# The head of a fused attention kernel: the first weight block in two transfers, the token rows ahead of the last two blocks, half a product of zeros less

## What is computed

```python
def _rmsnorm(x, g):
    y = x32 * lax.rsqrt(jnp.mean(x32 * x32, axis=-1, keepdims=True) + RMS_EPS)
    return (y * g).astype(x.dtype)

xn = _rmsnorm(x, norm_pre)                      # x: 520 rows of 1024
(qa, kvc, kvs, kvw, gn, ga, qd, kvd, krp, gb, ma, mb) = jnp.split(xn @ w_in, IN_OFFSETS, axis=-1)
...
cmp_past = cache_nsa_cmp[l, page_table]         # 8 x 4096 cached rows of 256 keys and values
kc, vc = _compress(jnp.concatenate([cmp_past, kvc], axis=1), pe_cmp)   # means over blocks of 32 rows
```

## Time and profile before

| | before |
|---|---|
| median of 3 runs | 666.37 us (666.15 to 666.65) |
| profiled execution | 666.29 us |
| its span | 664.5 us |
| PE busy | 650.8 us (98%) |
| DVE busy | 446.0 us (67%) |
| ACT busy | 214.4 us (32%) |
| POOL busy | 77.6 us (12%) |
| moved by DMA | 179.44 MB, mean 270 GB/s |

### The profile page before, as it was taken

The page is one execution under the profiler, slowest core; times in us unless marked ns, Lnnn a source line. Parts: engine busy times, 40 slices in busy tenths (PEclk is TensorE's granted clock), DMA queues, the critical chain, the costliest instruction groups (busy, mean ns, idle before and its releaser), DMA issues.

```text
span 664.5 us, 15351 instructions
## 1 busy us (share of the span) xinstructions
PE 650.8 (98%) x5771; PEld 433.3 (65%) x5771; DVE 446.0 (67%) x1234; ACT 214.4 (32%) x586; POOL 77.6 (12%) x89
## 2 busy tenths in 40 slices
PE   8999999999999998999999999999999999999996
PEld 3444444463466775778777676688788888886443
DVE  2198799676677778866575664637585757648866
ACT  0311321686445455544453542421011111010221
POOL 0344334126000000220201000000000000000010
PEclk9999999999999999999999999999999999999998
DMA  8999999999989999978759789975411112018011
GB/s 332 417 425 422 423 427 403 353 379 273 366 277 381 400 399 412 408 276 326 279 177 373 276 318 359 406 270 222 159 64 64 64 49 78 1 70 343 3 64 63
DMA packets 67587, 179.44 MB, mean 270 GB/s; under 512 B 7513, under 2 KB 16498, under 8 KB 60218
## 3 DMA queue, kind: packets, MB, share of 16 engines
q1 hardware_dynamic: 56088, 125.14, 51.2%
q0 software_dynamic: 8640, 48.90, 18.2%
q10 hardware_dynamic: 2786, 4.42, 1.8%
HBM read 169.38 MB, written 12.72 MB: 274 GB/s over the span
## 4 chain that ended last, share of the span: by engine, by line
PE 88%; DVE 5%; DMA 3%; ACT 2%; issue 1%; SPq 1%; DVEq 0%; ACTq 0%
PE bank L1561 20%; PE bank L978 12%; PE bank L1398 9%; PE bank L1612 7%; PE bank L1259 5%; PE bank L1382 4%; PE bank L1285 4%; PE bank L1269 4%; PE bank L1367 4%; DMA projP<-x 3%; PE bank L1590 2%; PE bank L1142 2%; PE bank L1332 2%; PE bank L1342 1%; PE bank L1220 1%
## 5 line engine op out<-in xcount | busy, mean ns | idle before, releaser
L978 PE MATMUL bank<-W,XG 128*128 128x494 f32 x192 | 83.6, 580 | 0.7 <-DVE projP L1998 0.7
L1871 ACT ACTIVATE projP<-bank,projP 128x128 f32<-128x128 f32 (+3 forms) x96 | 49.8, 525 | 38.5 <-DVE projP L2354 37.8
L2657 DVE TENSOR_TENSOR projP<-projP,bank 128x260 f32<-128x260 f32 x81 | 32.6, 422 | 42.4 <-PE bank L1561 41.6
L1398 PE MATMUL bank<-W 128*128 128x260 f32 x256 | 60.3, 389 | 0.0
L1661 ACT ACTIVATE projP<-bank 128x128 f32<-128x128 f32 (+5 forms) x87 | 33.4, 392 | 82.2 <-PE bank L1561 47.7
L978 PEld LDWEIGHTS bank<-W,XG 128*128 128x128 f32 x192 | 35.2, 192 | 36.5 <-issue 35.0
L1398 PEld LDWEIGHTS bank<-W 128*128 128x128 f32 x256 | 47.3, 190 | 10.6 <-issue 3.5
L1661 ACT ACTIVATE W<-bank 128x512 f32<-128x512 f32 (+2 forms) x69 | 40.2, 582 | 38.3 <-PE bank L1021 13.3
L2354 DVE CUSTOM_DVE_ANT_0 bank<-bank,maskb 128x128 f32<-128x128 f32 (+3 forms) x96 | 45.6, 509 | 8.0 <-PE bank L1259 7.1
L1259 PE MATMUL bank<-W 64*128 64x128 f32 (+7 forms) x192 | 46.0, 466 | 0.7 <-ACT projP L1871 0.7
L821 POOL DMA_INDIRECT ring<-cmp,idxi x32 | 38.6, 1208 | 67.8 <-DVE VV L2065 48.1
(11 more groups left out here) (479 smaller groups left out, 1163.6 us busy)
## 6 DMA issues: line engine op xcount, KB each, us to landing
ring<-latent SPq DMA_DIRECT2D x168, 256.0 KB, 4.9
XG<-latent SPq DMA_DIRECT2D x56, 256.0 KB, 4.4
W<-w_gate SPq DMA_DIRECT2D x12, 1024.0 KB, 5.8
W<-w_attn SPq DMA_DIRECT2D x16, 494.0 KB, 12.2
W<-latent SPq DMA_DIRECT2D x20, 256.0 KB, 5.3
rope_rows<-ring SPq DMA_DIRECT2D x16, 256.0 KB, 4.4
ring<-win SPq DMA_DIRECT2D x8, 512.0 KB, 7.7
ring<-w_out SPq DMA_DIRECT2D x2, 2048.0 KB, 11.8
```

The costliest lines, as they stand in the source:

```text
L978: mm = pe.matmul(bank[2 * (u % 2) + n][:, 0:GW], XG[:, k * TOK + tl * P:k * TOK + (tl + 1) * P], w_part(half, k, n), start=(k == 0), stop= ...
L1398: mm = pe.matmul(bank[6][:, 0:HALF], gate_w[g % 2][:, at:at + P], X2[:, k * TOK + hf * HALF:k * TOK + (hf + 1) * HALF], start=(k == 0), st ...
L1871: act.activation(Pb[u % 4][:, 0:w], bank[u % 2][:, 0:w], ACT.Exp, bias=NMp[:, u:u + 1], scale=-1.0, accum_out=RSp[:, u:u + 1]).then_inc(S[ ...
L2657: dve.tensor_tensor(out, a, pair_bank(v, product)[:, 0:HALF], ALU.add).then_inc(S["z_by_dve"], 1)
```

## The change

It has four parts.

1. SP loads block 0 of the first half in two transfers, group 0 on `w_in0` and group 1 on a semaphore `apart_in`, and PE takes block 0 by columns: group 0 for both tiles, then, after a wait on `apart_in`, group 1 for both tiles. The other blocks keep their order.
2. SP issues `xtok` and `xdec` ahead of blocks 6 and 7.
3. The second product on zeros is 256 words wide and not 512.
4. The late rotary loads count on `apart_in` too (the old `rope_apart`), one step of 16 further on.

```diff
@@ rope_landed
-                eng.wait_ge(S["rope_apart"], 16 * (ROPE_APART.index(p2) + 1))
+                eng.wait_ge(S["apart_in"], 16 * (ROPE_APART.index(p2) + 2))
@@ SP
-                sp.dma_start(W[:, k * 2 * GW:(k + 1) * 2 * GW], t["w_attn"][:, k, 0:2 * GW]).then_inc(S[f"w_in{k}"], 16)
-            sp.dma_start(xtok.rearrange("p (t c) -> p t c", t=TILES), t["x"][0:SEQ].rearrange("(t p) c -> p t c", p=P)).then_inc(S["xtok_in"], 16)
-            sp.dma_start(xdec[0:DEC], t["x"][SEQ:TOK]).then_inc(S["xtok_in"], 16)
+                if k == 6:
+                    sp.dma_start(xtok.rearrange("p (t c) -> p t c", t=TILES), t["x"][0:SEQ].rearrange("(t p) c -> p t c", p=P)).then_inc(S["xtok_in"], 16)
+                    sp.dma_start(xdec[0:DEC], t["x"][SEQ:TOK]).then_inc(S["xtok_in"], 16)
+                if k == 0:
+                    sp.dma_start(W[:, 0:GW], t["w_attn"][:, 0, 0:GW]).then_inc(S["w_in0"], 16)
+                    sp.dma_start(W[:, GW:2 * GW], t["w_attn"][:, 0, GW:2 * GW]).then_inc(S["apart_in"], 16)
+                else:
+                    sp.dma_start(W[:, k * 2 * GW:(k + 1) * 2 * GW], t["w_attn"][:, k, 0:2 * GW]).then_inc(S[f"w_in{k}"], 16)
@@ PE, project_first
-                    for tl in range(2):
-                        for n in range(2):
-                            mm = pe.matmul(bank[2 * tl + n][:, 0:GW], XG[:, k * TOK + tl * P:k * TOK + (tl + 1) * P],
-                                           w_part(0, k, n), start=(k == 0), stop=(k == KM - 1))
-                        if k == KM - 1:
+                    for tl, n in ((0, 0), (1, 0), (0, 1), (1, 1)) if k == 0 else ((0, 0), (0, 1), (1, 0), (1, 1)):
+                        if (k, tl, n) == (0, 0, 1):
+                            pe.wait_ge(S["apart_in"], 16)
+                        mm = pe.matmul(bank[2 * tl + n][:, 0:GW], XG[:, k * TOK + tl * P:k * TOK + (tl + 1) * P],
+                                       w_part(0, k, n), start=(k == 0), stop=(k == KM - 1))
+                        if k == KM - 1 and n == 1:
                             mm.then_inc(S["p1"], 1)
@@ PE, ahead of project_first
-            for _ in range(2):
-                pe.matmul(bank[7][:, :], VV[:, 0:P], VV[:, 0:512], start=True, stop=True)
+            for width in (512, 256):
+                pe.matmul(bank[7][:, 0:width], VV[:, 0:P], VV[:, 0:width], start=True, stop=True)
```

More of the change, by code:

```diff
@@ L1817, in load_rope @@
                     act.wait_ge(S["rope_out1"], 128)
-                act.dma_start(rope_home(p2), rope_rows[p2 * P:(p2 + 1) * P]).then_inc(S["rope_apart" if p2 in ROPE_APART else "kr_landed"], 16)
+                act.dma_start(rope_home(p2), rope_rows[p2 * P:(p2 + 1) * P]).then_inc(S["apart_in" if p2 in ROPE_APART else "kr_landed"], 16)
             group_copied(act, 15)
```

## The result

| | before | changed |
|---|---|---|
| median of the first measurement | 666.51 us (4 runs) | 675.79 us (4 runs, 673.31 to 680.66) |
| ratio, 95% interval | | 1.0128 [1.0086, 1.017] |
| median of a second one (experiment 12) | 665.96 us (11 runs) | 671.78 us (7 runs, 670.71 to 679.79) |
| ratio, 95% interval | | 1.0074 [1.0049, 1.01] |
| profiled execution | 666.29 us | 674.48 us |

The forecast was 668.3 us with a range up to 669.9. The direction and the mechanism came out as forecast. The size did not: the medians differ by 5.8 and 9.3 us and not by 2.0. The ratios are those on record with their intervals; they are not the quotients of the medians (1.0087 and 1.0139), so read them as one estimate and the medians as another. The changed kernel scatters by 7 to 9 us.

What follows compares the result with a forecast made beforehand. PE's list was taken as the path, with DMA full for the first 115 us. Late gathers eat the head's 1.1 us gain and leave PE 2.0 us behind: 666.29 + 2.0 = 668.3 us, range 666.4 to 669.9.

Steps and rivals of the forecast that it cites:

- The row that decides: POOL's first gather waits for block 7; with block 7 landing at 25.1 it is issued at 26.0, not 20.87.
- The stall at the first eviction: PE's 0.85 us wait before project(2) at 34.06, claimed to go once the token rows come earlier.
- 1 to 3: Expected profile sign: PE waits about 1 to 3 us for DVE at the second average, near 56 to 58.
- the head's gain holds: Rival: the gathers keep in time, idle time under 1.5 us or so, and the run takes 665.2; chance 0.10.
- slow clock at the second average: Rival: a 2 us wait there could lower PE's clock, giving 669.5 to 671; chance 0.10 together with longer idle time.
- I take 3.8: DMA engines idle from 24.3 until the first gather packets: 3.2 to 4.5 us, taken as 3.8.
- The sum had stretched 3.8 to 5.8 us for the 13th gather: q0 moves 0.55 of 0.85 MB beside the second weight half, so the gather lands at 73.1 to 74, not 67.3.
- the 2.8 us that I read from the earlier trace: Time from POOL's first gather issue (20.87) to first packet on q0 (about 23.7); the other bound was 1.5 us.
- the forecast's own step: At the fifth average PE takes the 20th fold, ended at 96.7, at about 96.8 against 94.84: 2.0 us behind.
- Sum on PE's head: 0.25 + 0.85 = 1.1 us: PE's start: 0.25 us from an earlier block 1 start plus 0.85 us of first eviction stall removed.
- The rotary table ... 5.5 us of cover of which 2 are used. Then PE is dense to the end: Late loads: table lands at 142.95, DVE reads it at 148.41, so no further loss; PE's 2.0 us stays.
- 1.5 to 2 us if the whole of block 0 runs so: Clock rival's price at the head: with fewer zeros, block 0's products run at 1.2 GHz; chance 0.10 with longer idle.

Runs made afterwards that it cites:

- experiment 12: The changed kernel as it is, timed and profiled once more against the kernel before: 671.78 us, ratio 1.0074.
- experiment 3: The whole change, with POOL's first gather waiting for block 5 and not block 7, against the kernel before: 667.19 us, 1.0005.
- experiment 4: The kernel before, with POOL also waiting for the token rows before its first gather and no transfer moved: 673.57 us, 1.009.
- experiment 6: The kernel before with token rows ahead of blocks 6 and 7 and the first gather waiting for block 5: 665.91 us, 0.9987.
- experiment 7: The kernel before with token rows ahead of blocks 6 and 7, gathers waiting for block 5, second zeros product 256 words: 666.79 us, 0.9995.
- experiment 8: The whole change, with w_qup and w_k issued ahead of the second rope_out, against the kernel before: 670.57 us, 1.0065.
- experiment 5: The kernel before with token rows ahead of blocks 6 and 7 and the first gather waiting for block 6: 673.85 us, 1.0092.
- experiment 1: The kernel before with only the token rows moved ahead of blocks 6 and 7: 673.93 us, 1.0104.
- experiment 9: The whole change, w_qup and w_k ahead of the second rope_out, second average three blocks later, against the kernel before: 672.44 us, 1.0069.
- experiment 11: The kernel before with only w_qup and w_k issued ahead of the second rope_out: 667.3 us, 0.9998.
- experiment 10: The kernel before with token rows ahead of blocks 6 and 7, gathers waiting for block 5, w_qup and w_k before second rope_out: 665.53 us, 0.9969.
- experiment 2: The kernel before with only block 0 split and taken by columns; token rows last, zeros whole: 667.39 us, 0.9998.

## Why the prediction failed in size

**What held.** The row that decides was the right one: the first gather waits for block 7, forecast for 26.0 and found at 26.79; the empty stretch was forecast at 24.5 to 28 and found at 25.4 to 28.5. The stall at the first eviction went. PE waits for folds at the second average, 2.7 us for the "1 to 3" forecast. Experiments 3 and 4 show this cause from both sides. The rival "the head's gain holds" needed an idle time under 1.5 us, which never came; with the gathers early (3, 6, 7) PE leaves the head 0.2, 0.4 and 1.3 us ahead, and the times stay within their noise of before. The rival "slow clock at the second average" came true in the first trace, on top of the forecast and not in place of it.

**The term mis-sized first: "I take 3.8" of idle time.** The idle time itself was not too short: the engines stop at about 25.3, and the first packets of the gather come at 28.5, 1.7 us after its issue, so 3.2 us, the lower end that I had given. Three things were missing beside it. The gathers start slowly: of the 0.73 MB by which the lag grows from 28.0 to 35.0 us, 0.21 belong to the last 0.5 us of idle time, and 0.52 to this, 1.2 us of transfer. The hardware queue ebbs before it is empty: from 21.0 to 25.4 us the lag grows by 0.37 MB, 0.9 us. And the split cost 0.17 MB, 0.4 us. The lag is 3.2 + 1.2 + 0.9 + 0.4 = 5.7 us, where the sum worked with 3.8. The sum had stretched 3.8 to 5.8 us for the 13th gather, by the share of q0; by the same share 5.7 us give 8.8, and the 13th is used 8.2 us late (75.53 against 67.33). The Trainium skill puts the first byte of a gather at about 1 us (DMA: Bandwidth & Descriptors, "Specifications"); 1.7 us with 1.0 us of issue in it is nearer to it than to the 2.8 us that I read from the earlier trace rows, where q0 had to share with a full q1. None of my rows had the slow start. That fewer gathers stand issued at the start, one and not four, is the difference at hand; no run shows it as the cause.

**What follows from it.** The 16th fold ends at 86.2 (forecast 84.2) and the 20th at 98.7 (forecast 96.7). By the forecast's own step PE can take the 20th at 98.7 to 98.8 in place of 94.84, which is +3.9 and not +2.0. The second trace of the changed kernel shows just that, +3.9. The rule was right and its input 2 us short. At the second average PE was already 3.2 us behind, above the 2.0 that the sum took from the fifth.

**The step on the head: "Sum on PE's head: 0.25 + 0.85 = 1.1 us".** The 1.1 us never came: PE goes into `project(2)` 0.44 us behind in the first trace and 0.67 in the second (34.73). The sum had block 1 unmoved at 8.55 and the second half at about 5.5. They landed at 10.1 and 6.57. The first 7.9 us moved 0.24 MB less than before (the sums of the two rows of GB/s). I had counted bytes; a row of half a block is 1976 bytes and not 3952, and block 0 takes two such rows for each one. The traces show the loss with the split; that the size of the rows makes it, and not the second issue, is argued. The split costs the head 1.1 us on average (experiment 7), as much as the whole gain forecast for it. So the first eviction came at 33.1 and not at 31.4, and DVE's first fold at 33.79 and not 1.5 us early. Here this didn't set the result, because the averages waited anyway.

**The step that failed: "The rotary table ... 5.5 us of cover of which 2 are used. Then PE is dense to the end".** I checked one transfer of SP's shifted chain and not the one ahead of it. `w_k` lands just when it is wanted. (SP's transfers are q1 in the profile; ACT's are a queue of their own, q10.) Of the ten traces without the edit of experiment 8, ACT waits for it in seven, and in the four with the edit in none. In six of those seven the copy follows the issue by 11.07 to 11.33 us; in the seventh by 13.7. The forecast's own numbers, a chain 4 us late and PE 2, would have shown it: without cover, the difference of the two is a wait. Measured, the issue is 6.1 us late and PE 4.5, and ACT waits 1.74. In experiment 4 it is 4.7 and 3.5, and ACT waits 1.28; in 5 it is 4.1 and 1.2, and ACT waits 3.09; in 1 it is 5.2 and 5.7, and ACT doesn't wait.

**The term left out of the sum: what a wait does to the clock.** The forecast had it as a rival of 0.10 together with another. In the first trace the slow passes cost 1.36 us (3.16 behind becomes 4.52), in experiment 5 more than 4, in experiment 12 about 3.7. Behind seven waits of 2.2 to 5.1 us (the changed kernel's two traces and experiments 1, 4, 5, 8, 9) the granted clock fell to between 0.50 and 0.56, and so it did behind two "issue" gaps of 2.3 and 2.6 us (4, 3). Behind waits of 1.4, 1.8 and 1.9 us, behind one of 2.7, and behind gaps up to 2.0 us it stayed at 1.00. Once, in experiment 7, it fell with no wait ahead, so a wait is not its only occasion. The Trainium skill (TensorE: Matmul & The Clock Gate, "What's actually happening") calls throttled the default state that activity lifts; the traces agree for nine of these ten waits and gaps of 2.2 us and more, and at the head, where I feared it, they show no loss with 2.93 us of zeros. (The price that I gave there, "1.5 to 2 us if the whole of block 0 runs so", was too low by my own numbers: its eight passes would take 6.6 us in place of 3.3.)

**The sum, as it should have stood** for the first trace: +3.2 at the second average, +1.4 of slow passes, +1.5 for `w_k`, and 2.2 between there and the end, 1.5 of it at the gap near 407 and 0.7 near 277. The forecast had 2.0 for the first and nothing for the other three. The first three give 666.3 + 6.1 = 672.4, which is the second measurement's 671.8 within its scatter.

**What stays open.** The gaps called "issue" belong to no part of the change: 2.0 us at 407.5 here, 2.3 at 406 in experiment 4, 2.6 at 274 in 3, 1.8 at 401 in 11, 1.5 at 413 in 12, and 0.5 at 399 in the kernel before. What makes one long was not found. The profile has a queue q8 of instruction loads, and a packet of it goes at 405.1 us here, just before the gap begins at 405.5, at 404.0 in experiment 4 and at 398.8 in 11, each less than a microsecond ahead of its gap. At 274 in 3 the last one went 2.5 us before. So a late load of instructions is a rival that no run tested. It was not found either why `w_k` took 13.7 us once. The two measurements of the changed kernel, 1.0128 and 1.0074, have intervals that overlap only from 1.0086 to 1.01; with a second wait between 1.8 and 5.1 us and a clock that may fall behind it, single executions differ by 8 us. In both measurements the slowest run has the lowest mean clock (0.990 and 0.989, the others 0.994 to 0.997). That this alone explains the difference is argued and not shown.

## What to carry to other kernels

When a load is moved up in a queue, look for who waits for the loads that it passes: here a semaphore of the last block also opened another queue, and the cure was to hang that wait on an earlier block. While DMA bounds a stretch, an empty slice is paid for in full and more, since the old stream ebbed before it and the new one started slowly behind it; measure the lag in bytes once the new stream is at its pace and not by the empty time. When a chain shifts, write down issue, landing and use of every transfer in it, not of one: the margin that breaks is the smallest, and of ten waits and gaps of PE of 2.2 us and more in these traces nine were followed by passes at the low clock, so that they were paid for more than once.

## What the runs showed of the hardware that I had not expected

- A stream of gathers that started on empty DMA engines, 1.7 us after its first issue, moved 0.22, 0.34 and 0.43 MB in its first three microseconds and 0.31 to 0.38 in each of the next four, in the changed kernel; experiments 1 and 4 began alike. Behind a full hardware queue (experiments 3, 10) the rate never fell under 400 GB/s from 24.5 to 35 us.
- One load of 128 rows of 3952 bytes cut into two of 1976 bytes delayed the load two places behind by 1.5 us (block 1 from 8.55 to 10.1; in experiment 2 PE took it at 10.49). Over all traces the products behind block 2 began 1.1 us later with the split.
- The granted clock of TensorE fell to about 0.50 in or behind nine single waits and gaps of 2.2 to 5.1 us in the midst of dense work, and came back some 3 to 9 us after the work went on. After one such wait of 2.7 us it did not fall, and once it fell for 3 to 4 us with no wait ahead (experiment 7).
